# Attention with the division moved behind the value sums, in a two-block kernel on one core

## The reference

```
s    = einsum('bqkgd,bskd->bkgqs', q, k) / sqrt(64)      # 512 queries x 768 keys, 8 heads
pr   = softmax(s, axis=-1)
o    = einsum('bkgqs,bskd->bqkgd', pr, v)
attn = o * silu(p[..., ZA_LO:ZA_HI])                     # the gate za
out  = concatenate([attn, conv]) @ w_out
```

## Time and profile before

| | us |
|---|---|
| three runs | 1159.25, 1159.65, 1155.62 |
| median | 1159.25 |
| profiled execution | 1152.58 |
| its span, first to last instruction | 1150.8 |
| TensorE (matmul) busy | 1070.5 (93%) |
| VectorE busy | 660.6 (57%) |
| ScalarE busy | 431.9 (38%) |
| GpSimd busy | 12.0 (1%) |

### The profile page before, as it was taken

How to read it: one execution, slowest core, us unless ns; L and a number is a source line. 1 busy time by engine, 2 the same in 40 slices (tenths; PEclk the granted TensorE clock), 3 DMA queues, 4 the chain that set the end, 5 groups by cost and what they waited for, 6 DMA issues and landing times.

```text
span 1150.8 us, 21841 instructions
## 1 busy us (share of the span) xinstructions
PE 1070.5 (93%) x9476; PEld 820.4 (71%) x9476; DVE 660.6 (57%) x1035; ACT 431.9 (38%) x701; POOL 12.0 (1%) x13
## 2 busy tenths in 40 slices
PE   6799999788997888999998989999999999999998
PEld 4377877465575667777676766678888888888887
DVE  2578899987355576667675826565444222444232
ACT  3333354557533642424333313444443211344121
POOL 0000000000000000000000000000000000000000
PEclk9999999999998989999999999999999999999999
DMA  8841322400032120010110004023222333232330
GB/s 345 319 130 60 104 73 73 148 1 1 19 120 82 51 79 21 21 39 21 39 39 21 21 2 185 3 77 107 92 92 93 109 92 102 87 104 92 110 101 28
DMA packets 25581, 94.93 MB, mean 82 GB/s; under 512 B 2832, under 2 KB 2832, under 8 KB 24976
## 3 DMA queue, kind: packets, MB, share of 16 engines
q1 hardware_dynamic: 25488, 93.54, 24.5%
HBM read 89.34 MB, written 4.19 MB: 81 GB/s over the span
## 4 chain that ended last, share of the span: by engine, by line
PE 57%; DVE 4%; ACT 2%; issue 1%; ACTq 0%; DVEq 0%
PE psum L698 14%; PE psum L699 14%; PE psum L700 14%; PE psum L708 4%; PE psum L1006 2%; PE psum L1019 1%; PE psum L1055 1%; PE psum L974 1%; PE psum L1022 1%; PE psum L1098 1%; PE psum L1089 1%; DVE work L2098 1%; PE psum L996 1%; PE psum L1078 1%; PE psum L928 1%
## 5 line engine op out<-in xcount | busy, mean ns | idle before, releaser
L1697 DVE TENSOR_TENSOR weights_low<-ring,weights_high 128x1024 fp32r<-128x1024 f32 x72 | 88.3, 1226 | 75.0 <-ACT weights_high L1351 75.0
L1351 ACT ACTIVATE weights_high<-ring 128x1024 fp32r<-128x1024 f32 x72 | 75.7, 1052 | 127.5 <-PE psum L700 127.5
L1304 ACT ACTIVATE work<-psum 128x384 f32<-128x384 f32 (+2 forms) x125 | 58.5, 515 | 113.0 <-PE psum L1055 48.9
L698 PE MATMUL psum<-normed_high,weights_high 128*128 128x512 f32 x256 | 100.2, 391 | 0.2 <-DVE weights_low L1697 0.2
L700 PE MATMUL psum<-normed_high,weights_low 128*128 128x512 f32 x256 | 99.7, 390 | 0.0
L699 PE MATMUL psum<-normed_low,weights_high 128*128 128x512 f32 x256 | 99.7, 390 | 0.0
L700 PE MATMUL psum<-hidden_high,weights_low 128*128 128x512 f32 x256 | 99.7, 389 | 0.0
L698 PE MATMUL psum<-hidden_high,weights_high 128*128 128x512 f32 x256 | 99.7, 389 | 0.0
L699 PE MATMUL psum<-hidden_low,weights_high 128*128 128x512 f32 x256 | 99.7, 389 | 0.0
L698 PE MATMUL psum<-pair_normed_high,pair_weights_high 128*128 128x512 f32 x176 | 77.2, 439 | 12.2 <-DVE normed_low L1702 4.2
L1622 DVE SCALAR_TENSOR_TENSOR work<-work,small_sb 128x512 f32<-128x512 f32 x116 | 80.1, 745 | 0.0
(11 more groups left out here) (239 smaller groups left out, 2059.0 us busy)
## 6 DMA issues: line engine op xcount, KB each, us to landing
ring<-weights SPq DMA_DIRECT2D x154, 512.0 KB, 3.6
residual<-xT SPq DMA_DIRECT2D x1, 2048.0 KB, 18.6
residual_saved<-residual SPq DMA_DIRECT2D x8, 256.0 KB, 2.0
residual<-residual_saved SPq DMA_DIRECT2D x1, 2048.0 KB, 9.0
outT<-residual SPq DMA_DIRECT2D x8, 256.0 KB, 3.2
work<-memT SPq DMA_DIRECT2D x1, 1024.0 KB, 5.0
work<-ctxT SPq DMA_DIRECT2D x1, 1024.0 KB, 9.9
small_sb<-small SPq DMA_DIRECT2D x1, 907.0 KB, 7.9
```

What stands on the lines that cost most here:

```text
L698: pe.matmul(out, wh, high(k), start=first and n == 0, stop=False)
L1304: free_inc(act.activation(out, bank(name, w) if src is None else src, ACT.Copy), name)
L1351: act.activation(WH[group(q)][:, q % 2, :], ring[:, SLOT[b], :], ACT.Copy).then_inc(w_high, 1)
L1697: vec.tensor_tensor(WL[group(q)][:, q % 2, :], ring[:, SLOT[b], :], WH[group(q)][:, q % 2, :].bitcast(F32), ALU.subtract).then_inc(w_low, 1)
```

## The change

The exponentials are no longer divided. VectorE still takes the reciprocals of the row sums, but keeps those of all steps (`INVERSE`, 32 columns) and raises `inverse_ready`. For each pair of heads, TensorE makes a tile `spread{j}` in which all 64 rows of a head hold the inverses of its 512 queries: eight fp32 matmuls whose stationary operand is one column of `INVERSE` repeated 64 times and whose moving operand is the identity. VectorE multiplies this tile into `CAT[:, j]` for the first three pairs, after their gating; for the last pair it multiplies it into the gate `ZA[:, 3]` before the gating. Spread 0, 1 and 2 are issued at the end of steps 9, 12 and 14, in bank 7, and VectorE's multiplications stand in steps 10, 13 and 15 behind the reciprocal. Spread 3 is issued in the last turn of the loop (u = 18), ahead of the last value sums, in bank 2. The turns now wait for the exponentials themselves.

```diff
+SPREAD_AT = {9: 0, 12: 1, 14: 2}
+assert not set(SPREAD_AT) & set(BESIDE_ATTENTION)
+BESIDE_ATTENTION.update({u: (f"spread{j}", 0, CK) for u, j in SPREAD_AT.items()})
...
+        if u == STEPS + VALUE_LAG - 1:
+            o.append((f"spread{NQ - 1}", 1, 2))
         if u in BESIDE_ATTENTION and BESIDE_ATTENTION[u][1] == 0:
...
-        SMALLT = sb("small_temps", P, 112)
+        SMALLT = sb("small_temps", P, 112 + 2 * STEPS)
...
+        INVERSE = SMALLT[:, 112:112 + 2 * STEPS]
...
+            def spread_inverse(j):
+
+                out = take(f"spread{j}")
+                pe.wait_ge(inverse_ready, QT * (j + 1))
+                for qt in range(QT):
+                    for h in range(2):
+                        i = 2 * (QT * j + qt) + h
+                        ins = pe.matmul(out[h * DH:(h + 1) * DH, qt * P:(qt + 1) * P],
+                                        INVERSE[:, i:i + 1].to_broadcast([P, DH]), tab("ident"), start=True, stop=True)
+                full_inc(ins, f"spread{j}")
...
             def turn_probs(t, h):
 
-                pe.wait_ge(probs_scaled, 2 * t + h + 1)
+                pe.wait_ge(*is_free(f"s{t}_{h}"))
...
+                if u == STEPS + VALUE_LAG - 1:
+                    spread_inverse(NQ - 1)
                 if v >= 0:
...
             for k in OUT_ORDER:
+                if k < NQ - 1:
+                    act.wait_ge(*is_free(f"spread{k}"))
                 act.wait_ge(*is_free(f"o{k}" if k < NQ else f"pw{k - NQ}"))
...
-            def divide_pair(u):
+            def invert_pair(u):
 
                 for h in range(2):
                     vec.wait_ge(*is_free(f"s{u}_{h}"))
                 i = 2 * u % 4
-                link(vec.reciprocal(ROWINV[:, i:i + 2], ROWSUM[:, i:i + 2]))
-                for h in range(2):
-                    probs = PR[(2 * u + h) % PROBS]
-                    vec.tensor_scalar(probs, probs, ROWINV[:, i + h:i + h + 1], None,
-                                      ALU.mult).then_inc(probs_scaled, 1)
+                vec.reciprocal(INVERSE[:, 2 * u:2 * u + 2], ROWSUM[:, i:i + 2]).then_inc(inverse_ready, 1)
+
+            def times_inverse_sums(j, x):
+
+                vec.wait_ge(*is_full(f"spread{j}"))
+                ins = vec.tensor_tensor(x, bank(f"spread{j}"), x, ALU.mult)
+                free_inc(ins, f"spread{j}")
+                return ins
...
                 if 1 <= u <= STEPS:
-                    divide_pair(u - 1)
+                    invert_pair(u - 1)
+                if u - 1 in SPREAD_AT:
+                    j = SPREAD_AT[u - 1]
+                    vec.wait_ge(*is_free(f"o{j}"))
+                    times_inverse_sums(j, CAT[:, j, :])
...
+            times_inverse_sums(NQ - 1, ZA[:, NQ - 1, :])
+            vec.wait_ge(*is_free(f"spread{NQ - 1}"))
             gated_heads(NQ - 1)
```

More of the change, by code:

```diff
@@ L515, in build @@
         negmax, probs_scaled = sem("negmax_ready"), sem("probs_scaled")
+        inverse_ready, last_gate = sem("inverse_sums_ready"), sem("last_gate_scaled")
         conv_out, conv_sq, conv_rs, conv_ln, conv_act = map(
@@ L820, in beside_attention @@
                     modulation_turn("gate", MODROW[0])
+                    return
+                if name[:6] == "spread":
+                    spread_inverse(int(name[6]))
                     return
@@ L917, in memory_unit @@
                 if 0 <= v < MUNITS:
-                    pe.wait_ge(probs_scaled, 2 * STEPS + v + 1)
+                    pe.wait_ge(probs_scaled, v + 1)
                     turn(f"et{v}", MT, MPR[:, v % (MAHEAD + 1), :])
```

## The result

The changed kernel took 1167.34 us (median of 15, 1155.47 to 1172.73), the kernel before 1159.25 (median of 15). The ratio is 1.0067, interval 1.0046 to 1.0087: 0.7% slower, where 0.4% faster was forecast. The profiled execution of the changed kernel took 1169.96, span 1168.1, so the two spans lie 17.3 us apart where the medians lie 8.1 apart; each profile is from its own end of its kernel's executions.

What follows compares the result with a forecast made beforehand. TensorE (93% busy) bounds the kernel; attention steps follow a scores-maximum-exponential ring, VectorE or TensorE. 5.3 us gained by scores 15 less 1.0 for the last spread saves 4.3: 1152.58 to 1148.3, or 1155 on the median; range 1147 to 1159.5.

Steps and rivals of the forecast that it cites:

- All that the change touches lies there: Claim that the change acts only in the attention stretch, 196.60 to 319.70 us, with no other gain taken behind it.
- The sum for the attention: Attention step by step, each the longest of ring, VectorE and TensorE: 5.3 us earlier less 1.0, so 4.3 saved.
- Scores 7: Attention score products starting step 7: expected 2.7 us nearer to scores 2, 25.5 instead of 28.2.
- Step by step: Attention steps, two heads of 128 queries each: length set by the scores-maximum-exponential ring, VectorE or TensorE, whichever is longest.
- Steps 13 and 14: Attention steps with the convolution's swish between VectorE and ScalarE, 7.88 and 7.74 us before: shorter by 2.2 together.
- The spread, taken at 1.0: Eight fp32 matmuls on TensorE in the attention, priced from the value sums' pace: 1.0 us each, four spreads.
- Spread 2 is hidden in step 14: Attention step 14: the spread falls in TensorE's 1.30 us wait for ScalarE's exponentials and costs nothing.
- the bank in steps 10 and 15: Products there wait for VectorE's multiplication to free the shared bank; in step 10 it holds by 0.25 us.
- A shift of the attention's end shifts all that follows by as much: The 831 us behind the attention start with the first output tile and move with it, no other gain taken.
- The slower one: Rival: the spreads' matmuls do not overlap, 4.4 us each; 8.9 us slower, 1168; chance 0.08.
- Halves in turn: Rival: the column halves of a spread take turns, 1.95 us each; 0.9 us saved, 1158.4; chance 0.15.
- All of VectorE's time arriving: Rival: VectorE's removed time all shortens the attention, net 13 us, 1146; chance 0.14.

Runs made afterwards that it cites:

- e1: Kernel before with 32 unused words added to the small temporaries, moving tiles behind them 128 bytes; median 1166.88 us, ratio 1.0077.
- e2: Changed kernel with the 32 columns of inverses placed behind all other tiles, so the others lie as before; median 1154.56 us, ratio 0.9988.
- e7: Changed kernel with small temporaries grown by 64 words in place of 32, a 256-byte shift; median 1154.40 us, ratio 0.9985.
- e11: e7 plus idle matmuls ahead of the last value sums (1.1 us planned, 1.4 in the profile); median 1151.79 us, ratio 0.9955.
- e12: e7 with spread 1 issued in step 13 in place of step 12; 1154.41 us, ratio 0.9978.
- e5: Kernel before with every tile moved by 16 words (64 bytes), distances between tiles kept; median 1156.76 us, ratio 0.9992.
- e3: Kernel before with 64 unused words (256 bytes) added to the small temporaries; median 1157.41 us, ratio 0.9987.
- e6: Kernel before with 8 unused words (32 bytes) added to the small temporaries; median 1166.50 us, ratio 1.0077.
- e4: Kernel before with 16 unused words (64 bytes) added to the small temporaries; median 1165.95 us, ratio 1.0072.
- e13: Kernel before with 0.6 us of idle matmuls ahead of the last value sums; median 1161.49 us, ratio 1.0030.

## Why the prediction was wrong

*The step that failed* is in its first part: "All that the change touches lies there." The change also makes the small temporaries 32 words longer. The line stands in the diff, and I priced it at nothing, without a word on it. It is worth 7 to 8 us (e1: median 8.3 above before; ratio 1.0077, 1.0053 to 1.0100) and turns the sign.

*The sum for the attention was right*, 4.3 forecast and 4.48 measured (109.06 less 104.58, e2 and e7), against the same profile of before that it was worked out from. Scores 7 are 25.5 us behind scores 2, as forecast. Step by step, length in us:

| step | 2 | 3 | 4 | 5 | 6 | 7 | 8 | 9 | 10 | 11 | 12 | 13 | 14 |
|---|---|---|---|---|---|---|---|---|---|---|---|---|---|
| before | 5.64 | 5.64 | 5.64 | 5.64 | 5.64 | 7.50 | 6.28 | 5.51 | 6.28 | 6.28 | 4.85 | 7.88 | 7.74 |
| forecast | 4.86 | 5.58 | 4.83 | 5.42 | 4.83 | 6.28 | 6.28 | 5.56 | 6.28 | 6.28 | 5.56 | | |
| e7 | 4.86 | 5.56 | 4.85 | 5.35 | 4.86 | 6.28 | 6.28 | 5.58 | 6.28 | 6.28 | 5.58 | 6.04 | 7.35 |

Steps 13 and 14 were forecast 2.2 shorter together and are 2.2. The spread, taken at 1.0 from the value sums, is 1.03 in steps 9 and 12 and 0.9 at the end. Spread 2 is hidden in step 14; TensorE does not wait for the bank in steps 10 and 15. The Trainium skill (TensorEngine Tiling (Array Packing), Key Properties) says that a change of tiling mode drains TensorE, which would have added a drain for each spread. The trace shows none: 0.80 from the start of the turn to that of the spread, as the earlier trace rows has it for other products.

*"A shift of the attention's end shifts all that follows by as much"* failed as well; the prediction named a change behind the attention as a sign that it is wrong. Behind the attention the same instructions take some us more or less, by the granted clock. With the layout mended, e2 and e7 should be at 0.996 and are at 0.9988 and 0.9985, with intervals that reach from 0.996 to 1.001. In the profile of e7, 4.3 us of the gain are lost again between the first output tile and the first memory scores (384.3 against 380.0) and 1.3 in the memory attention. For the changed kernel, 8.3 of layout less 4.5 of attention makes 3.8 of the measured 8.1 us; the rest, about 4 with an uncertainty of 2, I put down to the clock, from the 0.89 in its profile and its eight executions at the lower mean; that part is argued and not shown, since no run holds the clock fixed.

*The rivals.* The slower one gave 1168, and 1167 was measured, but for another reason: its spread of 4.4 us is refuted by 1.03. Halves in turn (1.95) is refuted too. All of VectorE's time arriving (13 us) is refuted by steps 8 to 11.

*The best version* is e7 with the delay of e11: 1151.79 against 1156.69, ratio 0.9955 (0.9937 to 0.9972). Of its gain only the attention's share is understood. e7 and e12 are the versions without idle work; at 0.9985 and 0.9978 neither can be told from the kernel before.

## What to carry to other kernels

When a diff changes the size of a tile, look up what is placed behind it, and keep the distance of TensorE's two operands as it was: round the change in size to 256 bytes, the one shift that cost nothing here. A bound worked out step by step for a stage says what the stage gives; before it is taken for the kernel's, compare the pace of the untouched stages, by starts of the same matmuls in both timelines. Where executions of one kernel spread by 1%, a gain of 0.4% is read from the timeline, and several executions' clocks are put beside it before anything is put down to the change.

## What the runs showed of the hardware

TensorE's pace hangs on the distance in a partition between the stationary and the moving operand. With 128x512 products that load new weights for every matmul (those of the MLP's first product), starts are 227 ns apart where the distance was kept or changed by 256 bytes (before, e5, e3), and 233 on the average where it changed by 32, 64 or 128 bytes (e6, e4, e1). The Trainium skill (TensorE: Matmul & The Clock Gate, Step-by-step: what each phase is for) says that loading the next tile's weights doesn't steal SBUF read bandwidth from the running matmul. If that held wherever the two lie, and nothing else about their places mattered, no distance would cost anything; here some cost 2.5%, and the measurement decides. That the cost comes from the two reads meeting in a bank is my reading of it, and no run shows it as such.

In a chain of small matmuls the granted clock can cost 7.5 us: the same 835 records of the memory attention took 61.41 at a mean clock of 0.89, against 53.90 at 1.00. How much of it falls behind the attention changes with small edits some 380 us earlier: with 0.6 us of idle work the whole came to 1.0030 of before (e13, 1.0007 to 1.0052; 56.64 at 0.94 in its profile), and 1.4 us took e7 from 0.9985 to 0.9955 (e11).
